# A two-block decoder kernel: head norms summed with tokens on the partitions, the turn table's last level shared by two engines, the output stored in eight parts

## The reference

```python
def rms_norm(x, gain):
    xf = x.astype(jnp.float32)
    y = xf * lax.rsqrt(jnp.mean(xf * xf, axis=-1, keepdims=True) + NORM_EPS)
    return (y * gain.astype(jnp.float32)).astype(x.dtype)

def memory_cross_attention(h, m, w_q, w_kv, q_norm, k_norm, w_o):
    q = rms_norm(to_heads(h @ w_q, XM_HEADS), q_norm)
    k, v = jnp.split(m @ w_kv, 2, axis=-1)
    k = rms_norm(to_heads(k, XM_HEADS), k_norm)
...
```

## Time and profile before

| | us |
|---|---|
| median of 3 runs (5091.86 to 5093.48) | 5092.28 |
| the profiled execution's own time | 5092.45 |
| its span, first to last instruction | 5090.7 |
| PE busy | 4680.0 (92%) |
| DVE / ACT / POOL busy | 2274.5 / 1431.5 / 1936.5 |
| mean granted TensorE clock, as a share of 2.4 GHz | 0.959 |

### The profile page before, as it was taken

One profiled execution on the slowest core, in us unless ns is written; L12 is line 12 of the kernel. 1 busy time (PEld: TensorE's weight loads), 2 busy tenths in 40 slices (PEclk: granted clock), 3 DMA queues, 4 the chain that ended last, 5 costly groups with the idle time before them and its releaser, 6 DMA issues. The chain is left out here.

```text
span 5090.7 us, 51495 instructions
## 1 busy us (share of the span) xinstructions
PE 4680.0 (92%) x19788; PEld 3545.9 (70%) x19788; DVE 2274.5 (45%) x4548; ACT 1431.5 (28%) x2131; POOL 1936.5 (38%) x884
## 2 busy tenths in 40 slices
PE   7567879999999999999999988899999997787999
PEld 5224757888888888888788745668878873365787
DVE  7787445993333233333440253453233136654440
ACT  2202322334444211111321234332232232233321
POOL 3044413446666444444444400334444431022443
PEclk9788989999999999999999989999999999998999
DMA  3001312445555655555222200212222221011222
GB/s 117 21 25 37 108 37 96 134 137 168 172 178 178 193 190 186 190 188 181 91 96 95 94 23 15 83 65 93 95 91 95 95 83 37 17 58 50 91 94 80
DMA packets 212164, 519.23 MB, mean 102 GB/s; under 512 B 16848, under 2 KB 82640, under 8 KB 208976
## 3 DMA queue, kind: packets, MB, share of 16 engines
q1 hardware_dynamic: 127440, 448.82, 26.9%
q10 hardware_dynamic: 84480, 67.12, 4.2%
HBM read 446.66 MB, written 69.21 MB: 101 GB/s over the span
## 5 line engine op out<-in xcount | busy, mean ns | idle before, releaser
L187 POOL TENSOR_TENSOR ring_rounded<-ring,highs_rounded 128x1024 fp32r<-128x1024 f32 x687 | 1682.1, 2450 | 2756.0 <-ACT highs_rounded L181 2756.0
L370 PE MATMUL bank<-arena_rounded,ring_rounded 128*128 128x512 f32 (+1 forms) x4488 | 1783.8, 397 | 97.3 <-DVE hT_rounded L388 41.4
L372 PE MATMUL bank<-arena_rounded,highs_rounded 128*128 128x512 f32 (+1 forms) x4488 | 1781.9, 397 | 0.0
L181 ACT ACTIVATE highs_rounded<-ring 128x1024 fp32r<-128x1024 f32 x687 | 727.8, 1061 | 2104.6 <-PE bank L372 1610.1
L371 PE MATMUL bank<-hT_rounded,highs_rounded 128*128 128x512 f32 x3128 | 1228.3, 393 | 0.0
L370 PEld LDWEIGHTS bank<-arena_rounded,ring_rounded 128*128 128x128 f32 x4488 | 854.1, 190 | 292.5 <-issue 86.2
L372 PEld LDWEIGHTS bank<-arena_rounded,highs_rounded 128*128 128x128 f32 x4488 | 852.5, 190 | 199.2
L371 PE MATMUL bank<-arena_rounded,highs_rounded 128*128 128x512 f32 (+1 forms) x2112 | 823.9, 390 | 0.0
L371 PEld LDWEIGHTS bank<-hT_rounded,highs_rounded 128*128 128x128 f32 x3128 | 593.3, 190 | 141.5
L371 PEld LDWEIGHTS bank<-arena_rounded,highs_rounded 128*128 128x128 f32 x2112 | 402.2, 190 | 91.0
L1207 DVE TENSOR_TENSOR arena<-qT,arena 128x512 f32<-128x512 f32 x64 | 150.6, 2354 | 372.2 <-ACT qT L1172 371.6
(11 more groups left out here) (319 smaller groups left out, 4727.7 us busy)
## 6 DMA issues: line engine op xcount, KB each, us to landing
ring<-pages_in SPq DMA_DIRECT2D x687, 512.0 KB, 3.4
act_table<-arena SPq DMA_DIRECT2D x128, 256.0 KB, 3.9
gate_table<-qT SPq DMA_DIRECT2D x16, 2048.0 KB, 7.3
arena<-act_table ACTq DMA_DIRECT2D x128, 256.0 KB, 3.9
arena<-gate_table ACTq DMA_DIRECT2D x32, 1024.0 KB, 8.6
arena<-ssm_in SPq DMA_DIRECT2D x16, 256.0 KB, 2.6
arena<-mem_in SPq DMA_DIRECT2D x3, 1024.0 KB, 4.8
xT<-x_in SPq DMA_DIRECT2D x8, 256.0 KB, 6.4
```

The source lines that it names most:

```text
L181: nc.scalar.activation(f32r(page_high(p)), slot(p), ACT.Copy).then_inc(masked_pages.sem, 1)
L187: nc.gpsimd.tensor_tensor(f32r(slot(p)), slot(p), part_of(page_high(p)), ALU.subtract).then_inc(split_pages.sem, 1)
L370: low_last = nc.tensor.matmul(out, f32r(w_low), f32r(x_high), start=start, stop=False)
L372: return low_last, nc.tensor.matmul(out, f32r(w_high), f32r(x_high), start=False, stop=stop)
```

## The change

Three parts. (1) `head_norm` sums with the squares as weights (128x128) and the window as two moving columns, for each block of 128 tokens, so that the sums stand with tokens on the partitions (128x4x16). Root and Newton run on that tile; four transposes and one ACT copy bring it back to one row for each head, and the spread reads those rows alone. ACT loads its root table at the block's start. Queries and keys of the memory and the cross attentions go into one stage, which leaves 8 of 11. (2) The table's last level (`m` = 256) leaves `turn_tables`: at the last four uses ACT makes eight products of 128x256 and DVE eight combinations, round by round. DVE starts the table earlier, while it waits for the norm. (3) The last `swiglu` stores each of its eight results as it is made. Smaller: the query projection of the cross attentions asks for its norm's sums one use earlier (`early=1`), and a wait for a small transfer moves to its first reader.

```diff
+        def upper_products(act, g):
+            act.wait_ge(shifted.sem, shifted.at(g + 1))
+            for t in range(4 * g, 4 * g + 4):
+                nc.scalar.activation(turned_part[2 * (t % 4)], sn(t)[:, 0:256], ACT.Identity, scale=sm[:, t:t + 1])
+                last = nc.scalar.activation(turned_part[2 * (t % 4) + 1], cs[:, t, 0:256], ACT.Identity,
+                                            scale=sm[:, t:t + 1])
+            last.then_inc(exped.sem, 1)
+        def upper_halves(dve, g):
+            dve.wait_ge(exped.sem, exped.at(g + 1))
+            for t in range(4 * g, 4 * g + 4):
+                nc.vector.scalar_tensor_tensor(out=cs[:, t, 256:512], in0=cs[:, t, 0:256], scalar=cm[:, t:t + 1],
+                                               in1=turned_part[2 * (t % 4)], op0=ALU.mult, op1=ALU.subtract)
...
+            last.then_inc(shifted.sem, 1)
-            while m < SEQ:
+            while m < SEQ // 2:
...
+                            if j == 0 and at_start:
+                                some(12.0)
                             dve.wait_ge(rooted.sem, rooted.at(ns))
...
+                            if at_start:
+                                some(4.0)
...
-                                if use >= 4 and (part[0] == "features" or b == 0):
+                                if upper is not None and use >= uses - 4:
+                                    if use == uses - 4:
+                                        some(1000.0)
+                                    upper[1](dve, use - uses + 4)
+                                elif beside is not None and use >= 1 and (part[0] == "features" or b == 0):
...
+                    nc.scalar.preload_act_table(ACT.Sqrt)
...
-                    nc.scalar.activation(rms, bank[0][0:32, 0:n], ACT.Sqrt, bias=gcol("eps")[0:32],
+                    nc.scalar.activation(r, sums, ACT.Sqrt, bias=gcol("eps"),
                                          scale=1.0 / width).then_inc(rooted.sem, 1)
+                    act.wait_ge(sent.sem, sent.at(1))
+                    nc.scalar.activation(by_head, bank[7][0:rows, :], ACT.Copy).then_inc(scaled.sem, 1)
...
-                            last = nc.tensor.matmul(bank[0][0:32, 0:n],
-                                                    mats[:, WINDOW, window + 30 - 2 * u:window + 62 - 2 * u],
-                                                    sq[:, u % 2, c, 0:n], start=(u == 0 and c == 0),
-                                                    stop=(u == count - 1 and c == len(chunks) - 1))
+                        for t in range(TB):
+                            tk = t % (long[u] // P) * P
+                            for c in range(len(chunks)):
+                                last = nc.tensor.matmul(sums[:, t, 2 * u:2 * u + 2], sq[:, u % 2, c, tk:tk + P],
+                                                        mats[:, WINDOW, window + 30:window + 32],
+                                                        start=(c == 0), stop=(c == len(chunks) - 1))
                         last.then_inc(summed.sem, 1)
+                    pe.wait_ge(inverted.sem, inverted.at(1))
+                    for t in range(TB):
+                        last = nc.tensor.transpose(bank[7][0:rows, t * P:t * P + P], r[:, t, :], mat(IDENT))
+                    last.then_inc(sent.sem, 1)
...
-                            nc.tensor.matmul(bank[1 + u % 3][:, 0:n], spread[:, u, :], small[:, 0:n], start=True,
-                                             stop=True).then_inc(full.sem, 1)
+                            some = whole if long[u] == SEQ else rows
+                            nc.tensor.matmul(bank[1 + u % 3][:, 0:long[u]], spread[0:some, u, :],
+                                             by_head[0:some, 0:long[u]], start=True, stop=True).then_inc(full.sem, 1)
...
-                    inverse_root(link, rms, bank[0][0:32, 0:n], 1.0 / width, EPS, newton[0:32, 0, 0:n],
-                                 newton[0:32, 1, 0:n])
+                    token_roots(link, (a, r, b), sums, width).then_inc(inverted.sem, 1)
...
-            head_norm([([Q(h)], ALL, f"xm_q_norm{layer}") for h in range(4)], SEQ, 128)
-            head_norm([([kT[:, h, 0:MEM]], ALL, f"xm_k_norm{layer}") for h in range(4)], MEM, 128)
+            head_norm([([Q(h)], ALL, f"xm_q_norm{layer}") for h in range(4)]
+                      + [([kT[:, h, 0:MEM]], ALL, f"xm_k_norm{layer}") for h in range(4)], 128)
...
+                    if store:
+                        for d in range(DC):
+                            sp.wait_ge(drawn.sem, drawn.at(d + 1))
+                            sp.dma_start(out[:, d, :], xT[:, d, :]).then_inc(stored.sem, 16)
+                        sp.wait_ge(stored.sem, stored.at(16 * DC))
...
-                sp.dma_start(out, xT[:]).then_inc(stored.sem, 16)
```

More of the change, by code:

```diff
@@ L350, in turn_tables @@
                 m *= 2
[L352 to L359, removed]
+            link.eng.sem_inc(shifted.sem, 1)
         def masked(out, x):
@@ L424, in project @@
         def project(src, high, nk, n, parts, by="act", norms=None, split=True, squares=None, early=2, keep=None,
-                    fetch=None, at_start=False, beside=None, budget=4.6, also=None):
+                    fetch=None, at_start=False, beside=None, budget=5.2, also=None, upper=None):
             first = page.start
@@ L441, in project @@
             tb_all = n // P
+            uses = sum(p[1] * (ns if p[0] == "features" else 1) for p in parts)
             def tok(j):
@@ L584, in _ @@
                             done += 1
+                        if upper is not None and use >= uses - 4:
+                            upper[0](act, use - uses + 4)
                         if norms is None and by == "act":
@@ L592, in _, with some @@
                     link = Dve(dve, dve_step)
+                    steps = beside(link) if beside is not None else iter(())
+                    def some(us):
+                        while us > 0:
+                            used = next(steps, None)
+                            if used is None:
+                                break
+                            us -= used
                     if norms is not None:
@@ L660, in project @@
                 exped.close(1)
-            uses = sum(p[1] * (ns if p[0] == "features" else 1) for p in parts)
+            if upper is not None:
+                exped.close(4)
+                shifted.close(5)
             full.close(uses)
@@ L671, in project, with head_norm @@
             page.start += count
-        def head_norm(units, n, width, rope=None, at=(0, 3584), newton=newton):
-            sq = arena[:, at[0]:at[0] + 2048].rearrange("p (b c n) -> p b c n", b=2, c=2)
-            spread = arena[:, at[1]:at[1] + 2048].rearrange("p (u f) -> p u f", u=16)
+        def head_norm(units, width, rope=None, at=0, roots=None):
+            sq = arena[:, at:at + 2048].rearrange("p (b c n) -> p b c n", b=2, c=2)
             rest = arena[:, 5632:6656].rearrange("p (b n) -> p b n", b=2)
-            rms = small[0:32, 0:n]
+            if roots is None:
+                roots = arena[:, 9472:9856]
             count = len(units)
+            long = [unit[0][0].shape[1] for unit in units]
+            rows = 2 * count
+            whole = 2 * sum(n == SEQ for n in long)
+            a, r, b = (roots[:, 128 * i:128 * i + 128].rearrange("p (t c) -> p t c", t=TB)[:, :, 0:rows]
+                       for i in range(3))
+            sums = bank[0][:, 0:128].rearrange("p (t c) -> p t c", t=TB)[:, :, 0:rows]
+            spread = arena[:, at + 2048 + 1536:at + 4096 + 1536] if at == 0 else arena[:, at + 2048:at + 4096]
+            spread = spread.rearrange("p (u f) -> p u f", u=16)
+            by_head = small[0:rows, 0:SEQ]
             with nc.Block() as block:
@@ L765, in head_norm @@
             loaded.close(16)
-            rooted.close(1)
-            inverted.close(1)
+            for s in (rooted, inverted, sent, scaled):
+                s.close(1)
             if rope is not None:
@@ L1811, in build @@
                                  ("tokens", TB, times_token(lambda t: V4[:, t, :])), ("features", 4, times(U))],
-                norms=normed(X, "norm_mix_g", DM, DC), squares=room(14592), at_start=True, beside=turn_tables)
+                norms=normed(X, "norm_mix_g", DM, DC), squares=room(14592), at_start=True, beside=turn_tables,
+                upper=(upper_products, upper_halves))
         head_norm([([Q(c)], PAIR, "att_q_g") for c in range(4)]
-                  + [([K(c)], PAIR, "att_k_g") for c in range(4)], SEQ, 64, at=(10496, 12544),
-                  newton=hT[:, 4:6, :])
+                  + [([K(c)], PAIR, "att_k_g") for c in range(4)], 64, at=10496, roots=hT[:, 4, 0:384])
         keep = lambda c: hT[:, c, :]
```

63 lines of the change are left out of this document (27 added, 36 removed).

## The result

The changed kernel takes 5163.2 us (median of 4 runs, 5161.34 to 5163.87), against 5092.07 for the kernel before in the same comparison: a ratio of 1.0139 [1.0122, 1.0157], 71 us slower. The profiled span is 5159.5 us instead of 5090.7, the mean clock 0.934 instead of 0.959. 5140 was forecast.

The account below looks back on a forecast made before the run. PE was taken to set the end, so only stretches where it waits can be shortened by other engines. Head norms +71, table -19 and store -4 gave +48 us on 5092.45, thus 5140, range 5065 to 5165.

Parts of the forecast that it names:

- chains of 5 us: Upper bound for the way from sums to spread in each of eight stages, 5 us instead of 4.1; total -30 us.
- a table that returns nothing: Rival: DVE's table rounds wait for ACT, the block ends at 166 as before, kernel at 5159 us; chance 0.07.
- Sums: Head-norm sums on PE: 672 instructions 0.215 us apart at clock 0.50, 144.5 us instead of 81.7, +63 us.
- Sums to spread: Root, Newton, transposes and copy between sums and spread: 4.1 us in each of eight stages, 33 us instead of 70.5, -38.
- The table load: ACT's root table loaded at each head norm's start, ahead of the squares PE waits for: 8 x 1.28, +10 us.
- Spreads: Head-norm spreads on 8 to 32 rows stay at clock 0.50, 3.44 us a unit with rotation: +36 us.
- Table: Turn table's last level made in four ACT and DVE rounds of 27 us, ending about 147 instead of 166: -19 us.
- Store: Output stored in eight parts at the kernel's end, only the last 256 KB left to land: -3.8 us.
- The other stretches: nothing: All stretches outside the head norms, table and store were put at a change of 0 us.
- the one at 2.4 GHz: Rival: head norms run at the high clock because weight loads or plain busy time count; 5006 us, chance 0.15.
- a load takes its time whatever the clock: Rival: sum instructions stay 0.112 us apart even at 0.50, sums -6 us, kernel at 5071 us; chance 0.08.
- the spreads would recover: Rival: sums at 0.50, but the clock comes back in the spreads, making them -23 us; 5103 us, chance 0.14.

Follow-up runs that it names:

- wide: The kernel after, but each sum product moves all 128 columns of the window tile instead of two (sums not those of the heads): 5104.19 us, ratio 1.0028.
- pairs: The kernel after with PE's order in stages with rotation changed to two spreads, then two rotations, instead of one and one: 5122.77 us, ratio 1.0061.
- wide_best: The kernel after with 128-row spread, 128 moving columns in the sums, all sums kept, and no early load of ACT's table: 5013.12 us, ratio 0.9849.

## Why the prediction was right, and where it was off

It forecast slower by 48 us, for the reason that the runs bear out: sums and spreads at a clock of 0.50. That the measured time lies in the range is in part luck. 5163 is 2 us below its upper end, which was set by chains of 5 us and a table that returns nothing, and neither happened. By its own steps:

- **Sums: right.** The pitch was taken as 0.215 us at clock 0.50; it is 0.216 (13.81 us for 64). +63 forecast, +59 measured, since in three stages the clock falls only after the sums have begun (0.54 to 0.65 over them). The choice of 0.50 rested on the earlier trace rows, and the run with 128 moving columns shows it: the same loads at 0.90.
- **Sums to spread: right.** 4.1 us a stage were forecast, 3.5 to 4.6 measured, -38 against -38.8.
- **The table load: mis-sized in the account.** It costs its 1.28 us in each stage, as forecast. But the row shows -4: three stages' own waits for squares, 6 us, go with the merging, which I had put into the spreads, and `early=1` takes 3.3 off in each cross attention, some of which comes back in the projection ahead of it.
- **Spreads: the clock right, the product too short.** This is the failed term. "With rotation PE does two products a unit, 3.44 at 0.50" is 4.01: each product alternates between 32 or 16 rows and 128 and pays 0.28 for a load in the open, a cost that the sum put at nothing without a reason. 67.3 us instead of 57.9 in MLA, 35.3 instead of 30.4 in the eight-unit stage, 24 us in all, of the 28.5 by which this term was too low, and as much as lies between 5140 and 5163, since the other errors cancel. Nearly all of the rest, 4.5, lies in the memory and cross attentions and `diff_subln`, which were put at nothing. I had given the term no bound above. The trace of before had the price, inside the very stretch of the earlier trace rows that was read for its clock (199.6 to 216.6), where products on 64 rows stand beside transposes on 128:

```profile
199.97 2.07 PE L808 MATMUL bank<-kT,qT 64*128 64x512 f32 x2
201.98 0.69 PE L818 MATMUL bank<-mats,hT 128*128 128x128 f32 x2
```
The product of 512 columns takes 2.01 us up to the next one at 0.50, not 1.72. In MLA's attention the same product has 128 rows, and beside the same transposes it takes 1.70 (4356.03 to 4357.73 in the kernel after, also at 0.50).
- **Table: right in the total, by two errors that cancel.** -18.5 against -19, or -19.8 without the ACT table load that stands in the same row. The levels up to 128 ended at 114.5, not 119, and the four rounds took 30.6 us (114.62 to 145.24), not 27, since two of them held a page of POOL's. ACT and DVE take turns as forecast. One sign failed: PE was to be idle for about 39 us ahead of the first sums and was for 19.74. The last four uses wait for DVE, which takes out their banks between the rounds, so PE's own work ended at 128.5 instead of 108.9. This cost nothing, as DVE ended last.
- **Store: right**, -4.0 against -3.8 for the whole last stretch.
- **"The other stretches: nothing": off by 10.** 8 of it lie between `diff_subln` and the cross attention, most of them where the stick-breaking part starts at a clock of 0.63 over its first 20 us, against 1.00 with the old head norms.

```profile
3081.00:3101.00 20.00, 20.00 (x52) 11.56 (x52) 2.31 (x6) 9.37 (x24) 0.00 (x0) 0.63 0.00 0
```
```profile
3046.78:3066.78 20.00, 19.70 (x78) 11.77 (x78) 3.93 (x8) 13.12 (x33) 0.00 (x0) 1.00 0.00 1
```
The first is the kernel after, the second the one with table and store alone: a low clock is handed on to the next stage.

Of the rivals, the one at 2.4 GHz and the one in which a load takes its time whatever the clock fell with `wide`. That the spreads would recover beside the 128-row rotation did not happen in the order of the change, but did, in part, in `pairs`: the rival was a change of order away. Its sum was wrong too: +63, -38, +8, -23 and -23 for table and store make 5079, not 5103, so half of its chance should not have gone to slower; with that half the chances given for slower add up to 0.66, not the 0.62 stated. The run with 128 rows has what it supposes, sums at 0.50 and spreads that recover, and took 5091: from spread to the next product it needs 162.2 us, 2 less than before and not 23. Each of its spreads begins at 0.50; where they begin at 1.00, as in `wide_best`, it is 149.0, 15 less. In the earlier trace rows two slices, not three, are below 7 tenths; nothing hangs on it.

The Trainium skill, "TensorE: Matmul & The Clock Gate", Part 1, says the clock gate watches how busy PE is. At equal busy time these runs have 0.50 and 0.90, so taken as the busy time of a profile that doesn't hold here.

## What to carry to other kernels

A product that does less (two columns, 32 rows instead of 128 with zeros) is not cheaper for TensorE when it takes the clock with it: look at the granted clock of the stretch, and at the clock of the stage behind it, before counting columns. Turning the sums round was a good idea for the engines that wait for them and a bad one for PE; padding what moves kept the first and undid the second. With the early table load left out, 150 us lie between two kernels that compute the same. When products of different row counts must alternate, group them: in MLA that gave 20 us a stage, in the eight-unit stage 2.6. And look for a price in the stretches you already read: the cost of a change of rows stood in one that was opened for its clock alone.

## What the runs showed of the hardware

- With the same loads and PE busy throughout, sums with two and with 32 moving columns had a clock of 0.50, with 128 columns 0.90 (27.47, 27.51 and 16.80 us for 128 instructions).
- Rows that hold zeros count as rows: the spread over 32 rows had 0.53, over 128 rows, 96 of them zero, 0.88, over the same stage. In the first head norm, where no product of other rows stands between, it was 0.50 with 16 rows and 0.83 with 128.
- Between a product on 32 or 16 rows and one on 128 the fp32 weight load isn't hidden: 0.27 to 0.29 us at 0.50 and 0.19 at 1.00, for each change; between 64 rows and 128 it is 0.29 at 0.50 (before). The same load is hidden where neighbours have equal rows. The Trainium skill, "TensorE: Matmul & The Clock Gate", Part 3, says loads for row groups that don't conflict, or for the background weight buffer, are pulled ahead of running products. 32 rows and 128 share a group, and the load waits; but neighbours of equal rows share theirs too, and there it runs ahead. So the row groups alone don't explain it, and no run here shows which buffer a load goes to.
- The order alone moved the clock: two and two instead of one and one, with the same products, gave 0.79 instead of 0.53 over the MLA spread (32 rows), and 0.60 instead of 0.50 over that of the eight-unit stage (16 rows), where it rose only at the end.

What stays open: why the order does it (the share of time on 128 rows is the same at a given clock, the exposed loads are fewer), why it does so much less with 16 rows, and why the unchanged stretch from the first attention to the memory's sums takes 450.6 us in one kernel and up to 458.9 in others.
